# A two-block transformer kernel: the order of its first loads and of its first turned chunks

## What is computed

```
def rmsnorm(x, g):
    xf = x.astype(jnp.float32)
    y = xf * lax.rsqrt(jnp.mean(xf * xf, axis=-1, keepdims=True) + NORM_EPS) * g.astype(jnp.float32)
    return y.astype(x.dtype)
...
h = rmsnorm(x, norm_mix[layer])
(q, kc, vc, ks, vs, kw, vw, nsa_g, rq, rk, rv, rg, gate_a, gate_b) = jnp.split(
    h @ w_in[layer], offsets, axis=-1)
```

## Time and profile before

| | |
|---|---|
| median of three runs | 965.0 us |
| the profiled execution | 964.91 us |
| its span | 962.9 us |
| TensorE busy | 954.6 us, 99% |
| VectorE busy | 634.4 us, 66% |
| ScalarE busy | 520.4 us, 54% |
| DMA, mean over the span | 177 GB/s |

### The profile page before, as it was taken

One profiled execution on the slowest core, in us unless ns is written; L12 is line 12 of the kernel. 1 busy time (PEld: TensorE's weight loads), 2 busy tenths in 40 slices (PEclk: granted clock), 3 DMA queues, 4 the chain that ended last, 5 costly groups with the idle time before them and its releaser, 6 DMA issues.

```text
span 962.9 us, 16027 instructions
## 1 busy us (share of the span) xinstructions
PE 954.6 (99%) x6578; PEld 866.2 (90%) x6578; DVE 634.4 (66%) x824; ACT 520.4 (54%) x790; POOL 63.2 (7%) x113
## 2 busy tenths in 40 slices
PE   9999999999999999999999999999999999999997
PEld 7877889989998888989988899998998899999996
DVE  5768675777555555778857787786667466555554
ACT  6576554555444544566865574544555444444443
POOL 3000001001000000324000001100000010000001
PEclk9999999999999999999999999999999999999999
DMA  9974536456665556556464456555655346665661
GB/s 308 298 242 126 154 90 177 154 175 191 204 195 177 190 182 186 161 181 190 143 195 131 134 164 207 156 186 169 200 167 167 118 156 217 182 195 179 193 192 45
DMA packets 133544, 170.37 MB, mean 177 GB/s; under 512 B 5824, under 2 KB 97296, under 8 KB 133472
## 3 DMA queue, kind: packets, MB, share of 16 engines
q1 hardware_dynamic: 131408, 165.07, 55.4%
q10 hardware_dynamic: 1424, 2.84, 0.9%
q0 software_dynamic: 640, 1.44, 0.6%
HBM read 168.28 MB, written 1.05 MB: 176 GB/s over the span
## 4 chain that ended last, share of the span: by engine, by line
PE 94%; DMA 2%; DVE 2%; ACT 1%; issue 0%; POOLq 0%; DVEq 0%; POOL 0%; ACTq 0%
PE ps L374 15%; PE ps L375 15%; PE ps L376 15%; PE ps L405 7%; PE ps L407 6%; PE ps L406 6%; PE ps L737 5%; PE ps L738 5%; PE ps L736 5%; PE ps L357 5%; PE ps L461 3%; DMA raws<-in_w_in 2%; PE ps L494 1%; PE ps L492 1%; PE ps L493 1%; DVE parts L1561 1%
## 5 line engine op out<-in xcount | busy, mean ns | idle before, releaser
L1561 DVE TENSOR_TENSOR parts<-raws,parts 128x1024 fp32r<-128x1024 f32 (+2 forms) x307 | 367.4, 1213 | 220.2 <-ACT parts L1038 219.3
L1038 ACT ACTIVATE parts<-raws 128x1024 fp32r<-128x1024 f32 (+2 forms) x307 | 315.8, 1045 | 234.4 <-PE ps L376 133.9
L374 PE MATMUL ps<-room_r,parts 128*128 128x256 f32 x1248 | 351.7, 282 | 0.0
L375 PE MATMUL ps<-room_r,parts 128*128 128x256 f32 x1248 | 348.7, 279 | 0.0
L376 PE MATMUL ps<-room_r,parts 128*128 128x256 f32 x1248 | 348.4, 279 | 0.0
L374 PEld LDWEIGHTS ps<-room_r,parts 128*128 128x128 f32 x1248 | 234.6, 188 | 5.8 <-issue 4.3
L375 PEld LDWEIGHTS ps<-room_r,parts 128*128 128x128 f32 x1248 | 234.7, 188 | 1.3
L376 PEld LDWEIGHTS ps<-room_r,parts 128*128 128x128 f32 x1248 | 234.6, 188 | 0.0
L405 PE MATMUL ps<-parts,room_r 128*128 128x512 f32 (+1 forms) x336 | 134.3, 400 | 0.6 <-DVE parts L1561 0.6
L407 PE MATMUL ps<-parts,room_r 128*128 128x512 f32 (+1 forms) x336 | 131.0, 390 | 0.0
L406 PE MATMUL ps<-parts,room_r 128*128 128x512 f32 (+1 forms) x336 | 131.0, 390 | 0.0
(11 more groups left out here) (226 smaller groups left out, 887.3 us busy)
## 6 DMA issues: line engine op xcount, KB each, us to landing
raws<-in_w_in SPq DMA_DIRECT2D x99, 512.0 KB, 4.6
raws<-in_w_ffn_in SPq DMA_DIRECT2D x44, 512.0 KB, 4.3
raws<-in_w_up SPq DMA_DIRECT2D x32, 512.0 KB, 4.5
raws<-in_w_down SPq DMA_DIRECT2D x32, 512.0 KB, 4.5
raws<-in_w_ffn_out SPq DMA_DIRECT2D x22, 512.0 KB, 4.2
raws<-in_w_xkv SPq DMA_DIRECT2D x16, 512.0 KB, 3.9
raws<-in_w_out SPq DMA_DIRECT2D x8, 512.0 KB, 4.1
raws<-in_w_up_ssd SPq DMA_DIRECT2D x8, 512.0 KB, 5.7
```

Of the source, the lines that this page charges most:

```text
L374: e.matmul(ps, wh, hT[0][:, k, :], start=k == 0, stop=False)
L375: e.matmul(ps, wh, hT[1][:, k, :], start=False, stop=False)
L1038: e.activation(t.h, t.raw, ACT.Copy).then_inc(s["hi"], 1)
L1561: e.tensor_tensor(t.l, t.raw, t.h.bitcast(F32), ALU.subtract).then_inc(s["lo"], 1)
```

## The change

- SP's first load is x[:, 0:256] of both token tiles. Columns 256 to 511 follow behind weight tile 1, the second half behind tile 3. `ident` moves to the head of ScalarE's queue, and `cols` is loaded whole right behind it.
- The first block of `qkv` has depths 1, 1, 1, 1, 2, 2. Every later tile's number rises by one; `w1_behind` keeps its numbers.
- x is turned in chunks: one bank holds chunk k of both token tiles (two transposes, 256 columns). There are eight such banks. ScalarE rounds a bank straight into the high part, with the gain as the activation's per-partition scale; VectorE writes (bank x gain) - high part in one instruction. Both are 128x256. `big` is no longer used here. TensorE waits per chunk for VectorE's release of the bank.
- The zero matmuls between the first transposes and the first product go from five to three.
- The orders of ScalarE and VectorE at the start are: chunks 0, 1; tiles 0, 1; chunks 2, 3; tiles 2, 3; chunks 4, 5, 6, 7; tile 4; on ScalarE then the sums of token tile 0, tile 5, the sums of token tile 1.

```
--- before.py
+++ after.py
@@ SEMS
-    "x00", "x01", "x10", "x11", "gain", "ident", ...
+    "x_first", "x_second", "x01", "x11", "ident", ...
@@ tensor
             def x_ready(u):
-                return lambda k, t=1: need(s["xT"], 4 * u + (1 if k < 4 else 3) + t)
+                return lambda k, t=1: need(s["xT"], 4 * (u - 1) + (1 if k < 4 else 3) + t)
+
+            def first_ready(k, t=1):
+                out_of(("turn", MIX, k))
...
-            def x_half(q):
-                for t in range(2):
-                    need(s[f"x{t}{q}"], 16)
-                    turn_x(MIX, t, q)
+            def x_quarter(q, *loads):
+                for load in loads:
+                    need(s[load], 16)
+                for k in (2 * q, 2 * q + 1):
+                    turn(("turn", MIX, k), [x[:, t, P * k:P * k + P] for t in range(2)])
 
             idle(6)
-            x_half(0)
-            idle(5)
+            x_quarter(0, "x_first")
+            idle(3)
 
             w_in = a["w_in"][0]
-            units = tm("qkv", w_in, 0, 512, xT, x_ready(MIX), depths=[1, 1, 2, 2, 2])
+            units = tm("qkv", w_in, 0, 512, xT, first_ready, depths=[1, 1, 1, 1, 2, 2])
+            next(units)
+            x_quarter(1, "x_second")
             next(units)
             next(units)
-            x_half(1)
+            x_quarter(2, "x01", "x11")
+            x_quarter(3)
             run(units)
@@ scalar
-            e.dma_start(x[:, 0, 0:512], xin[:, 0, 0:512]).then_inc(s["x00"], 16)
-            e.dma_start(cols[:, 0:8], a["cols"][:, 0:8]).then_inc(s["gain"], 16)
+            e.dma_start(ident, a["ident"]).then_inc(s["ident"], 16)
+            e.dma_start(cols[:, :], a["cols"]).then_inc(s["cols"], 16)
...
-            rounds(MIX, 0, True, (0,))
-            round_tile()
-            rounds(MIX, 0, True, (1,))
+            def first_rounds(q):
+
+                for k in (2 * q, 2 * q + 1):
+                    e.wait_ge(s["pe"], where["turn", MIX, k].at)
+                    e.activation(xT[0][:, k, :], psum[:, where["turn", MIX, k].bank, 0:256], ACT.Copy,
+                                 scale=col("norm_mix")[:, k:k + 1]).then_inc(s["first_hi"], 1)
+
+            e.wait_ge(s["cols"], 16)
+            first_rounds(0)
             round_tile()
             round_tile()
-            e.dma_start(cols[:, 8:], a["cols"][:, 8:]).then_inc(s["cols"], 16)
+            first_rounds(1)
             round_tile()
-            rounds(MIX, 1, True)
             round_tile()
+            first_rounds(2)
+            first_rounds(3)
+            round_tile()
+            for load in ("x_first", "x_second", "x01"):
+                e.wait_ge(s[load], 16)
             for q in range(2):
-                e.wait_ge(s[f"x0{q}"], 16)
                 sum_of(x, 0, q, MIX)
             round_tile()
...
@@ vector
-            e.wait_ge(s["gain"], 16)
-            gains(MIX, 0, True)
-            rests(MIX, 0, (0,))
-            rest_of_tile()
-            rests(MIX, 0, (1,))
+            def first_rests(q):
+
+                for k in (2 * q, 2 * q + 1):
+                    name = ("turn", MIX, k)
+                    e.wait_ge(s["first_hi"], k + 1)
+                    emptied(stt(xT[1][:, k, :], bank_of(name)[:, 0:256], col("norm_mix")[:, k:k + 1],
+                                xT[0][:, k, :].bitcast(F32), ALU.mult, ALU.subtract), name)
+
+            first_rests(0)
             rest_of_tile()
             rest_of_tile()
-            gains(MIX, 1, True)
+            first_rests(1)
             rest_of_tile()
-            rests(MIX, 1)
+            rest_of_tile()
+            first_rests(2)
+            first_rests(3)
+            rest_of_tile()
@@ sync
-            e.dma_start(ident, a["ident"]).then_inc(s["ident"], 16)
-            e.dma_start(x[:, 1, 0:512], xin[:, 1, 0:512]).then_inc(s["x10"], 16)
+            e.dma_start(x[:, :, 0:256], xin[:, :, 0:256]).then_inc(s["x_first"], 16)
...
-                if t.i == 2:
+                if t.i == 1:
+                    e.dma_start(x[:, :, 256:512], xin[:, :, 256:512]).then_inc(s["x_second"], 16)
+                if t.i == 3:
                     for half_ in range(2):
                         e.dma_start(x[:, half_, 512:], xin[:, half_, 512:]).then_inc(s[f"x{half_}1"], 16)
```

## The result

The changed kernel took 970.92 us (median of 6 runs, 969.56 to 971.26) against 965.07 for the kernel before (6 runs, 964.46 to 965.70): a ratio of 1.006, interval 1.0050 to 1.0069. That is slower by 5.85 us. The forecast was 967.6 with a range of 965.2 to 969.6: right in sign, 3.3 us short, and outside its range. The profiled execution took 969.56, span 967.5, so 4.6 us more than the profiled one of before.

A forecast was written before the change was run, and what follows sets the result against it. TensorE bounds the kernel; its late start and order stalls shift k 4 by +3.3 us, of which the wait at `hidden` swallows about 0.6. Sum: 964.9 + 2.7 = 967.6 us, range 965.2 to 969.6.

The forecast's parts named there:

- What bounds the kernel: Whole kernel: TensorE, busy 99% of the span; its late start and later waits are paid in full.
- The wait ahead of `hidden`: Near 57 us: TensorE's wait of about 0.6 us for the windows swallows that much of a right shift.
- Start of x, columns, table load: Start: transposes at 4.0, `cols` landing at 5.0 at no cost, table load at 4.7 behind the turned chunk.
- rival B: Start: table load stays in front of both ScalarE waits, start -0.7, total +1.7, 966.6; chance 0.14.
- Chunk and tile steps: Start: first product at 8.15 instead of 7.87, then TensorE waits 0.7 before k 2 and 2.0 before k 4.
- tile 5 was hidden: After k 4: tile 5, behind two sums, is ready at 20.0 and needed at 20.7, so costs nothing.
- rival D: Before k 4: clock falls to its lower level in a gap, or loads come late; 969 to 970.4; chance 0.13.
- The DMA steps: Weight loads up to 37 us: later tiles stay hidden, and earlier w1 loads fill a queue hole; no cost.
- tile 13: Near 35 us: delayed 1.4 us by earlier w1 loads, lands at 33.5 to 35, just hidden with zero slack.
- E: Earlier w1 loads and shorter chunk steps give back 1 to 2 us: +0.5 to +1.5, 966; chance 0.07.
- C: Before k 4: no order stalls, k 4 at 14.2 to 15.2, some 963.9, faster; chance 0.08.

The follow-up runs named there:

- The order experiment: Changed kernel with tile 2 ahead of chunks 2 and 3, tile 4 ahead of chunks 4 to 7, on ScalarE and VectorE: 967.56 us.
- all three edits: Changed kernel with table load first, tiles ahead of chunks, and nine zero matmuls instead of three: 965.29 us, ratio 1.0002; two variants add to it.
- the three later executions: The changed kernel, nothing altered, run once each three more times: 969.40, 967.92 and 969.21 us.

## Why the prediction was wrong

**What bounds the kernel: right.** TensorE's late start and its waits were paid in full, and no other engine mattered. The wait ahead of `hidden` vanished as forecast, but it was 0.4 us and not the 0.6 that I took it for.

**Start of x, columns, table load: right.** The transposes began at 4.04 (forecast 4.0). `cols` with its 77 KB landed at about 5.0 (issued at 1.21, 3.8 us to landing; forecast 5.0), while the table load ran, so it cost nothing. The table load stood at 4.81 behind the turned chunk (forecast 4.7), ahead of the landing of `cols`; the forecast had this from one row of another place of the kernel, and rival B is out. The activation came at 6.11, 0.02 us behind the load, so of the 1380 ns of drain in the Trainium skill, page "ScalarE: Activation LUTs", section "What ACT_TABLE_LOAD costs", nothing is seen here either. The experiment with the load first shows its price on the path: 1.1 us.

**Chunk and tile steps: right.** First product at 8.24 (forecast 8.15); waits of 0.55 and 1.80 (forecast 0.7 and 2.0), each ended by the remainder that was named. The brackets count from the modelled end of the matmul before. Counted from one start to the next, as I had done, the waits are 0.72 and 1.97, the forecast's 2.7 in all. The order experiment removes them, and tile 5 was hidden after the change, as I had said, but not once TensorE came earlier.

**The step that failed: the clock, rival D's mechanism, which the sum left out.** I had written that "the idle time ahead of the first real matmul grows from 0.64 to about 1.7" and that "the gaps are short beside the work around them", and gave D 0.13. Two errors:

- The gap was 2.63 us, not 1.7. I had priced the six zero instructions at the low level to about 6.4. They ended at 5.61: the clock had risen by 4.8, so they followed each other at 0.11 us ((0.83 - 0.275) / 5) instead of 0.23, the distance in the first twelve ((2.93 - 0.42) / 11), and what the zero matmuls save adds to the gap. The mix of 275 and 421 ns in the kernel before showed only that the clock rises about there, not that it does so at a fixed time.
- I took a missing row for an argument: no gap of this length stands in the trace of before, so it showed nothing against a fall. The section of the Trainium skill that I had quoted, "HAM oscillation — how this bites in real kernels" on the page "TensorE: Matmul & The Clock Gate", pointed the right way, and three of the four traces of the changed kernel agree with it (0.50 from about 8.2 to 11.5).

Its term: k 2 came at 13.75 where I had 12.15, 1.6 later, and k 4 at 19.51 where I had 17.9, again 1.6. From the first product to k 2 the changed kernel takes 5.51 us and the one with twelve zero matmuls 4.05, so 1.46 of it is the clock's, a term that the sum had at nothing.

A second term was mis-sized by 0.25. Between k 4 and the windows the kernel after takes 42.35 us, where I had 42.1 (60.0 - 17.9). I had TensorE at the windows of before at 56.7, from 56.35 "plus two short steps"; in the kernel after the same two steps take 0.55 (61.31 to 61.86), so it would have been there at 56.9, and the wait that could swallow a shift was 0.4 us. So +2.7, +1.6 and +0.25 make the +4.5 at the windows. D's price of 2.8 us was that of twelve matmuls at the low level, while the last six of the twelve ran at the upper one (0.23 apart from 11.87 on) and the lower level cost 0.20 us a matmul (0.43 against 0.23), not 0.23. D as a sum, 969 to 970.4, holds the profiled execution, but not the median.

**The DMA steps and the other rivals.** No new wait appeared between 20 and 57 us, so tile 13 was not late, and the w1 loads put back behind their old tiles changed 0.2 us in the traces; E's give-back did not come. C asked for k 4 before 15.2. Only kernels with all three edits reach that (14.25 in the first), and even they are no faster than the kernel before.

**What stays open.** The four traced executions of the changed kernel took 967.92 to 969.56. Its other five took 970.19 to 971.26, with mean granted clocks of 0.993 to 0.997 beside 0.996 to 0.998 in the four, and have no trace. They lie 1.3 us on average above the slowest traced one and I can't say where. More of the low clock would fit four of them, but not the one of 971.21 with 0.997. So the forecast's 3.3 us of error in the median has two parts: some 2 us that the traces explain, nearly all of it the clock, and some 1.3 us that none of them shows. Whoever takes the three later executions as the measure has a loss of 4.5 us and no such rest. Open too is what, beside the gap, decides whether the clock falls.

## What to carry to other kernels

- When an edit puts a second wait ahead of an engine's first activation, the table load may end up behind it. An activation on data that is there anyway, placed first, brought back 1.1 us at the start, and 2.6 us at k 4 together with the clock.
- Count the zero matmuls in front of late work by what gap they leave if they run at full clock, not at the low one; the same six instructions took 0.83 or 1.49 us in one and the same program. A wait that is longer than any in the old trace is an unknown with a price on both sides, and the clock's part of it belongs into the range.
- In an order written by hand, ask at each step which of the two items TensorE needs first and which is there first. Chunks ahead of a tile that had landed cost 1.8 us; the tile ahead of the chunks cost some 0.5 us where the tile was late, beside the 0.8 that TensorE would have waited for the tile in any order.

## What the runs showed of the hardware that I had not expected

- Idle times of 2.0 and of 2.49 to 2.63 us ahead of the first product (six traces) were followed by 0.50 of granted clock for about 3 us; idle times of 0.36 to 1.25 and one of 1.81 there were not, nor were those of 1.80 to 1.82 ahead of k 4. What else enters into it than the idle time was not tested.
- After the gap of 2.63 us in the kernel after the clock was already down when work began; after the one of 2.0 it fell 1.5 us into the new work.
- The moment at which the clock first rises differs between executions of one program: the six zero instructions from 4.8 or 4.9 us on took 0.83 us in three traces and 1.49 in one. The granted clock reads 1.00 in that early stretch in all of them, though the instructions' durations (421 and 275 ns in the earlier trace rows) show two levels. Durations tell what the column does not.
- The size of the first column load cost little. The DMA issues of the kernel after:

```profile
cols<-in_cols ACTq DMA_DIRECT2D x1, 77.0 KB, 3.8
```

against 3.6 us for 4 KB. In the other traces of kernels with the 77 KB load it took 3.7 to 4.2 us.
